# Head 0 of an expert layer: the first eight experts searched and gathered by themselves, and eight scalings spread among the first rows

## The chip, the cores and the metric

The kernel runs on one core of a Trainium2 chip. The metric is the device time of one execution in microseconds; three executions of the kernel before gave a median of 1569.95.

## The reference, cut to what matters

One encoder block over 512 tokens of width 1024, all float32:

```
h   = x + W_out [ FoX attention || differential attention ]( W_in RMSNorm(x) )
hn  = RMSNorm(h)
q   = (hn @ w_q)  as 8 heads x 2 sides x 128
sc  = q against 128 sub keys of each head and side
s1, i1 = top_k(sc[side 0], 16);  s2, i2 = top_k(sc[side 1], 16)
cand   = s1[:, None] + s2[None, :]          (16 x 16 sums)
top_s, pos = top_k(cand, 16);  eidx = i1*128 + i2 at pos
hid = gelu(u_tab[eidx] . hn) * softmax(top_s)
h   = h + sum over 8 heads x 16 experts of hid * v_tab[eidx];  out = RMSNorm(h)
```

The best eight of the 256 sums can only be made of the best eight of each side (a sum at places i and j, counted from 1, has at least i*j sums that are no smaller). So an 8 x 8 table gives the first eight experts of a head, in order.

## The kernel before

The 512 tokens are four tiles of 128 (tokens on the partitions). Work runs in three stages.

1. Tile 0 goes through the attention block alone, up to the queries and keys of its first three heads (the list `BEFORE`).
2. The hosted stage: VectorE (DVE) works through tile 0's experts, 8 heads x 16, one 128x1024 dot product (`dot`, L1489) and one 128x1024 scaled addition (`add_row`, L1525) for each. Between them it does the pieces of the list `AFTER`: the remaining queries and keys of tile 0, and the whole attention block of tiles 1 to 3. TensorE (PE) and ScalarE (ACT) walk the same list. Each head has 4 groups of 4 experts and 9 gaps in a group; `share(p)` gives each piece a weight, and the running sum of weights sets its gap. ACT reaches the gelu of a group (`gelu`, L1138) at gap 6, behind every piece that stands earlier, so a gelu waits for the PE work of those pieces.
3. The last stage: tiles 1 to 3, 24 heads x 16 experts; every row of 8 KB per token (u and v side by side, 1 MB for 128 tokens) is gathered into a ring, DVE makes the dot products, and PE adds the rows (L946).

Expert rows come by indirect DMA that POOL issues (`gather_u` L656, `gather_v` L663, queue q0 of the profile), 512 KB for 128 tokens. The rings hold four u rows and four v rows: a gather of row c waits until row c-4 has been used. POOL issues u0 to u3, and then u4, v0, u5, v1 and so on. Weights come as slabs of 1 MB that SP issues (L597, queue q1) into a ring of two places; the slab after next is issued when the matmuls of a place's present slab are over. A slab of queries serves one head.

Head 0 has a start of its own on DVE: `hn_tile(0)`, then `topk_all(0, 0)` (the whole search of head 0, L1414 to L1474, `topk_first` and the nine parts of `topk_second`), then `later_cols()`: x of tiles 1 to 3, laid out by dimension, is scaled into `actT` by eight instructions of 128x384 (L1623). PE needs all eight (`cols_ready`) before the first projection of tiles 1 to 3 (L740). The searches of later heads lie between the rows of the head ahead.

POOL's first gather waits for the count `TK_IDX` of `topk_step`, which the last instruction of the search of the numbers (L1472, `eidx`) reaches.

Of the kernel before, what the change touches and what calls it, by code (L numbers as in the profile page):

```python
# [25 lines left out]
U32 = mybir.dt.uint32  # L26
ALU = mybir.AluOpType
# [51 lines left out]
def build(nc, x, x_cols, g1_cols, first_halves, slabs, f_cols, b_f, lambda_q1, lambda_k1, lambda_q2, lambda_k2, subln_g,  # L79
# [12 lines left out]
    SLAB = HALF_BANK  # L92
    CHUNK = 64
# [73 lines left out]
    def share(p):  # L167

        kind, tiles = p[0], len(GROUPS[p[1]]) if len(p) > 1 and p[0] != "attend" else 1
        if kind == "attend":  # L170
            _, g, half, step = p
            each = (len(items_of(half)) + VALUES_LAG) / (2 * len(items_of(half)))
            ends = [at_step(g, half, step), at_step(g, half, step - VALUES_LAG)]
            return sum(each * SHARE_ATTEND[e[0]] for e in ends if e)
        if kind == "outproj":
            return SHARE_ROWS[1]
        if kind in ("project", "query"):
            by_rows = in_rows(p[1], p[2]) if kind == "project" else tiles == 1
# [3 lines left out]
        return {"norm1": 4, "xT": 2, "forget": 6, "mix": 4, "mixT": 1, "turn": 1, "selq": 2, "norm2": 4, "hT": 2, "lambda": 1, "lamrow": 1, "squares": 0, "factors": 0, "keys": 1.0 * tiles}[kind]  # L182
# [77 lines left out]
    BEFORE, later = first_pieces[:cut_at], first_pieces[cut_at:] + pieces_of(1)  # L260
# [75 lines left out]
    with ExitStack() as ctx:  # L336
# [82 lines left out]
        eidx = [sb(f"eidx{i}", [P, TOPK], I32) for i in range(3)]  # L419
        gneg = sb("gneg", [P, 1])  # L420
# [87 lines left out]
        topk_step = sem("topk_step")  # L508
        gexp_done = sem("gexp_done")
# [131 lines left out]
        def _(pool):  # L641
# [43 lines left out]
            numbers_of(0)  # L685
            for c in range(COLS):
                gather_u(0, c)
            for n in range(PH * HOSTS):
                for c in range(TOPK):
                    ahead = TOPK * n + c + COLS  # L690
                    if ahead < HOSTED:
                        if ahead % TOPK == 0:
                            numbers_of(n + 1)
                        gather_u(ahead // TOPK, ahead % TOPK)
# [516 lines left out]
        def _(dve):  # L1211
# [32 lines left out]
            def piece(kind, *p):  # L1244
# [12 lines left out]
                elif kind == "factors":  # L1257
# [3 lines left out]
                    for t in range(later):  # L1261
                        nc.vector.tensor_scalar(factor_diag[:, t * P:(t + 1) * P], ident[:, :], stat1[:, 2 * later + t:2 * later + t + 1],
                                                None, ALU.mult).then_inc(factors_ready, 1)
                elif kind == "forget":
# [140 lines left out]

            def topk_first(n, par):
# [8 lines left out]
                for q in range(2):  # L1415
                    after(q + 1)
                    nc.vector.match_replace(tk_w[:, q, :], tk_v[:, q, 0:8], s1[q], -HUGE).then_inc(topk_step, 1)
                for q in range(2):
                    nc.vector.max_index(tk_i[:, q, 0:8], tk_v[:, q, 0:8], s1[q]).then_inc(topk_step, 1)
                for q in range(2):  # L1420
                    after(q + 3)
# [8 lines left out]
            def topk_second(n, par, part):  # L1430
# [37 lines left out]
                else:  # L1468
# [3 lines left out]
                    nc.vector.scalar_tensor_tensor(out=eidx[n % 3][:, :], in0=picked[:, 0, :], scalar=float(K1), in1=picked[:, 1, :],  # L1472
# [144 lines left out]
            def later_cols():  # L1617

                dve.wait_ge(cols_in, 16 * later)
                dve.wait_ge(*emptied(("factors",)))  # L1620
                rows = factor_rows.rearrange("p (t n) -> p t n", t=later)
                for c in range(KC):
                    nc.vector.scalar_tensor_tensor(out=actT[:, c, :].rearrange("p (t n) -> p t n", t=later),  # L1623
                                                   in0=v_all[:, 1:TILES, c * P:(c + 1) * P], scalar=g1c[:, c:c + 1], in1=rows,
                                                   op0=ALU.mult, op1=ALU.mult).then_inc(cols_ready, 1)

            hn_tile(0)
            topk_all(0, 0)
            later_cols()
# [89 lines left out]
```

## Time and profile before

| what | value |
|---|---|
| median of 3 executions (lowest, highest) | 1569.95 us (1568.25, 1570.33) |
| the profiled execution, its own time | 1568.42 us |
| its span in the profile | 1566.6 us |
| PE busy | 1256.3 us, 80% |
| DVE busy | 1142.4 us, 73% |
| POOL busy | 777.5 us, 50% |
| ACT busy | 431.6 us, 28% |
| DMA | 596.49 MB, mean 381 GB/s |

Times in the profile are counted from the start of the span; 1.8 us of the execution's time lie outside of it. Stage 1 ends at about 94 us, stage 2 at about 580 us. The busy shares are averages over stages with different limits.

### The profile page before, as it was taken

To read this page: it belongs to the slowest core of one execution; us is meant where nothing else is said; L and a number is where in the kernel's file an instruction comes from. 1 tells how busy PE (TensorE), PEld (TensorE's weight loads), DVE (VectorE), ACT (ScalarE), POOL (GpSimd) and SP (SyncE) were. 2 spreads that over 40 slices of the span, in tenths; PEclk is the share of its full clock that TensorE was granted. 3 is DMA by queue.
4 is the path that set the end of the run, shared out by engine and by line. 5 is a ranking of instruction groups with operands and counts; after the bars stand their busy time and mean duration, and the time that the engine had idled before them with its cause. 6 is when DMAs were issued, how large, how long until landed. Compare 5 with 4: busy or idle time off the path is not lost.

```text
span 1566.6 us, 12915 instructions
## 1 busy us (share of the span) xinstructions
PE 1256.3 (80%) x3663; PEld 655.4 (42%) x3663; DVE 1142.4 (73%) x2681; ACT 431.6 (28%) x1045; POOL 777.5 (50%) x650
## 2 busy tenths in 40 slices
PE   9988988897775928989987768687777777777777
PEld 8666654475452613444433323233333333333333
DVE  3357799999999888666676776767666776666664
ACT  3321334343441313222221222222222322222122
POOL 0025576776566773444454445444544454445540
PEclk9999988998787968999999989989999999989999
DMA  9479898998789999999999999999999999999994
GB/s 383 183 284 383 338 345 322 373 364 318 277 286 330 368 374 412 421 422 415 421 422 421 421 422 421 421 421 422 421 421 422 421 421 422 421 421 421 422 421 206
DMA packets 102045, 596.49 MB, mean 381 GB/s; under 512 B 11736, under 2 KB 11736, under 8 KB 46680
## 3 DMA queue, kind: packets, MB, share of 16 engines
q0 software_dynamic: 92160, 536.91, 85.2%
q1 hardware_dynamic: 9816, 58.76, 9.5%
q8 instruction: 31, 0.51, 0.1%
q14 instruction: 38, 0.31, 0.1%
HBM read 593.53 MB, written 2.10 MB: 380 GB/s over the span
## 4 chain that ended last, share of the span: by engine, by line
DMA 33%; DVE 15%; PE 12%; ACT 2%; issue 2%; POOL 1%; POOLq 0%; DVEq 0%
PE acc L946 11%; DMA map_mem<-in_peer_uv_dram,eidx 6%; DMA mix_mem<-in_peer_uv_dram,eidx 6%; DMA v_ring<-in_peer_uv_dram,eidx 5%; DMA u_ring<-in_peer_uv_dram,eidx 4%; DMA v_all<-in_peer_uv_dram,eidx 4%; DMA w_ring<-in_peer_uv_dram,eidx 3%; DMA act_mem<-in_peer_uv_dram,eidx 3%; DVE v_ring L1497 1%; PE mm L740 1%; DVE v_all L1497 1%; DVE map_mem L1497 1%; DVE u_ring L1497 1%; DVE onehot L1457 1%; DVE onehot L1463 1%
## 5 line engine op out<-in xcount | busy, mean ns | idle before, releaser
L656 POOL DMA_INDIRECT u_ring<-in_peer_u_dram,eidx x128 | 163.4, 1277 | 177.2 <-DVE gneg L1474 98.7
L1138 ACT ACTIVATE gel<-hid 128x4 f32<-128x4 f32 x126 | 26.1, 207 | 778.8 <-DVE hid L1497 694.9
L663 POOL DMA_INDIRECT v_ring<-in_peer_v_dram,eidx x128 | 154.9, 1210 | 76.5 <-DVE h L1525 44.6
L946 PE MATMUL acc<-v_all,diag 128*128 128x512 f32 x240 | 124.4, 667 | 68.1 <-ACT diag L1145 68.1
L1525 DVE SCALAR_TENSOR_TENSOR h<-v_ring,coef,h 128x1024 f32<-128x1024 f32 x128 | 164.5, 1285 | 7.2 <-DMA v_ring<-in_peer_v_dram,eidx 3.7
L1489 DVE CUSTOM_DVE_ANT_0 u_ring<-u_ring,hn 128x1024 f32<-128x1024 f32 x128 | 156.2, 1220 | 14.5 <-DMA u_ring<-in_peer_u_dram,eidx 12.6
L946 PE MATMUL acc<-v_ring,diag 128*128 128x512 f32 x240 | 116.6, 631 | 29.6 <-ACT diag L1145 29.6
L946 PE MATMUL acc<-u_ring,diag 128*128 128x512 f32 x240 | 116.9, 633 | 28.9 <-ACT diag L1145 28.9
L946 PE MATMUL acc<-map_mem,diag 128*128 128x512 f32 x240 | 113.7, 618 | 23.0 <-ACT diag L1145 23.0
L1145 ACT ACTIVATE diag<-ident,coef 128x128 f32<-128x128 f32 x376 | 121.7, 392 | 27.7 <-DVE coef L1515 21.7
L677 POOL DMA_INDIRECT v_all<-in_peer_uv_dram,eidx x60 | 70.7, 1178 | 92.7 <-PE acc L946 87.7
L740 PE MATMUL mm<-act_mem,w_ring 128*128 128x384 f32 x336 | 115.5, 500 | 0.7 <-ACT act_mem L1065 0.7
L677 POOL DMA_INDIRECT u_ring<-in_peer_uv_dram,eidx x60 | 72.1, 1201 | 86.7 <-PE acc L946 78.7
L677 POOL DMA_INDIRECT map_mem<-in_peer_uv_dram,eidx x60 | 71.0, 1184 | 83.4 <-PE acc L946 77.0
L946 PEld LDWEIGHTS acc<-v_all,diag 128*128 128x128 f32 x240 | 49.9, 213 | 137.3 <-issue 103.0
L1497 DVE CUSTOM_DVE_ANT_0 map_mem<-map_mem,hn 128x1024 f32<-128x1024 f32 x60 | 72.9, 1224 | 45.7 <-DMA map_mem<-in_peer_uv_dram,eidx 45.7
L677 POOL DMA_INDIRECT v_ring<-in_peer_uv_dram,eidx x60 | 70.6, 1176 | 70.7 <-PE acc L946 62.6
L946 PE MATMUL acc<-act_mem,diag 128*128 128x512 f32 x168 | 83.0, 640 | 25.2 <-ACT diag L1145 25.2
L1497 DVE CUSTOM_DVE_ANT_0 v_all<-v_all,hn 128x1024 f32<-128x1024 f32 x60 | 72.9, 1225 | 40.1 <-DMA v_all<-in_peer_uv_dram,eidx 40.1
L1497 DVE CUSTOM_DVE_ANT_0 u_ring<-u_ring,hn 128x1024 f32<-128x1024 f32 x58 | 70.4, 1223 | 41.4 <-DMA u_ring<-in_peer_uv_dram,eidx 41.3
L1497 DVE CUSTOM_DVE_ANT_0 v_ring<-v_ring,hn 128x1024 f32<-128x1024 f32 x58 | 70.3, 1224 | 38.4 <-DMA v_ring<-in_peer_uv_dram,eidx 38.3
L946 PE MATMUL acc<-w_ring,diag 128*128 128x512 f32 x168 | 77.9, 607 | 19.1 <-ACT diag L1145 19.1
(273 smaller groups left out, 2342.4 us busy)
## 6 DMA issues: line engine op xcount, KB each, us to landing
w_ring<-in_slabs_dram SPq DMA_DIRECT2D x37, 1024.0 KB
v_ring<-in_slabs_dram SPq DMA_DIRECT2D x6, 1024.0 KB, 10.8
u_ring<-in_slabs_dram SPq DMA_DIRECT2D x4, 1024.0 KB, 13.0
h<-in_x_dram SPq DMA_DIRECT2D x4, 512.0 KB, 12.9
u_ring<-in_peer_u_dram,eidx POOLq DMA_INDIRECT x128
v_ring<-in_peer_v_dram,eidx POOLq DMA_INDIRECT x128
v_all<-in_x_cols_dram SPq DMA_DIRECT2D x3, 512.0 KB, 6.6
out_dram<-fin SPq DMA_DIRECT2D x3, 512.0 KB
```

The costliest lines, as they stand in the source:

```text
L656: nc.gpsimd.indirect_dma_start(out=u_ring[:, c % U_RING, :], out_offset=None, in_=peer_u[0], in_offset=bass.IndirectOffsetOnAxis(ap=eidx[n ...
L663: nc.gpsimd.indirect_dma_start(out=v_ring[:, c % V_RING, :], out_offset=None, in_=peer_v[0], in_offset=bass.IndirectOffsetOnAxis(ap=eidx[n ...
L677: nc.gpsimd.indirect_dma_start(out=row_mem[place], out_offset=None, in_=peer_uv, in_offset=bass.IndirectOffsetOnAxis(ap=eidx[n % 3][:, c:c ...
L740: last = nc.tensor.matmul(bk[:, 0:n], w[:, c, q * P:(q + 1) * P], actT[:, c, 0:n], start=(c == 0), stop=(c == KC - 1))
L946: last = nc.tensor.matmul(acc[half][:, :], diag[:, c % COLS, :], v_row(n, c)[:, half * BANK:(half + 1) * BANK], start=first, stop=(n % PH ...
L1138: nc.scalar.activation(gel[:, par, g0:g0 + COLS], hid[:, par, g0:g0 + COLS], ACT.Gelu).then_inc(gelu_done, 1)
L1145: nc.scalar.activation(diag[:, c, :], ident[:, :], ACT.Copy, scale=coef[:, par, g0 + c:g0 + c + 1]).then_inc(diag_done, 1)
L1457: nc.vector.tensor_tensor(out=onehot[:, :, :], in0=top_hl[:, :, :].rearrange("p a b -> p (a b)").unsqueeze(2).broadcast_to([P, 2 * TOPK, T ...
L1463: nc.vector.tensor_tensor(out=oh, in0=oh, in1=tk_i[:, :, :].unsqueeze(2).broadcast_to([P, 2, TOPK, TOPK]), op=ALU.mult).then_inc(topk_step, 1)
L1489: nc.vector.tensor_tensor_reduce(out=u_ring[:, c % U_RING, :], in0=u_ring[:, c % U_RING, :], in1=hn[:, :], scale=1.0, scalar=0.0, op0=ALU. ...
L1497: nc.vector.tensor_tensor_reduce(out=u_row(n, c), in0=u_row(n, c), in1=hn[:, :], scale=1.0, scalar=0.0, op0=ALU.mult, op1=ALU.add, accum_o ...
L1525: nc.vector.scalar_tensor_tensor(out=ht, in0=v_ring[:, c % V_RING, :], scalar=coef[:, par, c:c + 1], in1=ht, op0=ALU.mult, op1=ALU.add).th ...
```

## The change

Three things are done.

- In `topk_first`, the search for the numbers of each side's best eight (`max_index`) moves ahead of `match_replace`, for every head; the counts of `topk_step` in the waits follow.
- For head 0 alone, `eight_first()` comes directly behind it: nine instructions on small tiles (an 8x8 table of sums, `max`, `max_index`, two splits of the position, a comparison, a product, a sum, and the numbers themselves) write `eidx[0][:, 0:8]` and raise `first_eight`. POOL's first gather waits for that; it waits for the full search only ahead of u8. The full search of head 0 then writes numbers 8 to 15 only.
- `later_cols()` goes. Its eight instructions are pieces `("cols", 1, i)` of weight 0, one behind each of the first eight pieces of the list `AFTER`. All other pieces keep their gaps.

```
-    BEFORE, later = first_pieces[:cut_at], first_pieces[cut_at:] + pieces_of(1)
+    BEFORE, later = first_pieces[:cut_at], []
+    for i, p in enumerate(first_pieces[cut_at:]):
+        later += [p] + [("cols", 1, i)] * (i < KC)
+    later += pieces_of(1)
...
-            numbers_of(0)
+            pool.wait_ge(first_eight, 1)
             for c in range(COLS):
                 gather_u(0, c)
             for n in range(PH * HOSTS):
                 for c in range(TOPK):
                     ahead = TOPK * n + c + COLS
                     if ahead < HOSTED:
+                        if ahead == EIGHT:
+                            numbers_of(0)
...
+                elif kind == "cols":
+                    g, c = p
+                    dve.wait_ge(cols_in, 16 * later)
+                    dve.wait_ge(*emptied(("factors",)))
+                    rows = factor_rows.rearrange("p (t n) -> p t n", t=later)
+                    nc.vector.scalar_tensor_tensor(out=actT[:, c, :].rearrange("p (t n) -> p t n", t=later),
+                                                   in0=v_all[:, 1:TILES, c * P:(c + 1) * P], scalar=g1c[:, c:c + 1], in1=rows,
+                                                   op0=ALU.mult, op1=ALU.mult).then_inc(cols_ready, 1)
...
+            def eight_first():
+
+                def sides(ap, last):
+
+                    return ap.unsqueeze(last).broadcast_to([P, EIGHT, EIGHT])
+
+                cf = first_cand[:, :, :].rearrange("p a b -> p (a b)")
+                link(nc.vector.tensor_tensor(out=first_cand[:, :, :], in0=sides(tk_v[:, 0, 0:EIGHT], 2), in1=sides(tk_v[:, 1, 0:EIGHT], 1),
+                                             op=ALU.add))
+                link(nc.vector.max(first_v[:, :], cf))
+                link(nc.vector.max_index(first_p[:, :], first_v[:, :], cf))
+                nc.vector.tensor_scalar(first_hl[:, 0, :], first_p[:, :], 3, None, ALU.logical_shift_right).then_inc(dve_chain, 1)
+                chain[0] += 1
+                link(nc.vector.tensor_scalar(first_hl[:, 1, :], first_p[:, :], EIGHT - 1, None, ALU.bitwise_and))
...
+                nc.vector.scalar_tensor_tensor(out=eidx[0][:, 0:EIGHT], in0=first_id[:, 0, :], scalar=float(K1), in1=first_id[:, 1, :],
+                                               op0=ALU.mult, op1=ALU.add).then_inc(first_eight, 1)
...
                 for q in range(2):
                     after(q + 1)
+                    nc.vector.max_index(tk_i[:, q, 0:8], tk_v[:, q, 0:8], s1[q]).then_inc(topk_step, 1)
+                if n == 0:
+                    after(4)
+                    eight_first()
+                for q in range(2):
                     nc.vector.match_replace(tk_w[:, q, :], tk_v[:, q, 0:8], s1[q], -HUGE).then_inc(topk_step, 1)
                 for q in range(2):
-                    nc.vector.max_index(tk_i[:, q, 0:8], tk_v[:, q, 0:8], s1[q]).then_inc(topk_step, 1)
-                for q in range(2):
-                    after(q + 3)
+                    after(q + 5)
...
-                    nc.vector.scalar_tensor_tensor(out=eidx[n % 3][:, :], in0=picked[:, 0, :], scalar=float(K1), in1=picked[:, 1, :],
+                    lo = EIGHT if n == 0 else 0
+                    nc.vector.scalar_tensor_tensor(out=eidx[n % 3][:, lo:], in0=picked[:, 0, lo:], scalar=float(K1), in1=picked[:, 1, lo:],
...
             hn_tile(0)
             topk_all(0, 0)
-            later_cols()
```

On DVE, at the head of head 0's search, the rows before were:

```order
L1532 SCALAR_TENSOR_TENSOR hn<-h,rstd,g2b 128x1024
L1414 MAX tk_v<-store 128x8 x2
L1417 MATCH_REPLACE tk_w<-tk_v,store 128x128 x2
L1419 MAX_INDEX tk_i<-tk_v,store 128x8 x2
L1422 MAX tk_v<-tk_w 128x8 x2
```

and in the changed kernel they are (L1434 to L1448 are `eight_first`):

```order
L1459 MAX tk_v<-store 128x8 x2
L1462 MAX_INDEX tk_i<-tk_v,store 128x8 x2
L1434 TENSOR_TENSOR first_cand<-tk_v 128x64
L1436 MAX first_v<-first_cand 128x8
L1437 MAX_INDEX first_p<-first_v,first_cand 128x8
L1438 TENSOR_SCALAR first_hl<-first_p 128x8
L1440 TENSOR_SCALAR first_hl<-first_p 128x8
L1441 TENSOR_TENSOR first_hot<-first_hl,iota_i 128x128
L1445 TENSOR_TENSOR first_hot<-first_hot,tk_i 128x128
L1447 TENSOR_REDUCE first_id<-first_hot 128x16
L1448 SCALAR_TENSOR_TENSOR eidx<-first_id 128x8
L1467 MATCH_REPLACE tk_w<-tk_v,store 128x128 x2
```

Nine instructions have come in, and the remaining search of head 0 stands behind them.

On DVE, at the end of that search and among the first four dot products (`u_ring`), the rows before were:

```order
L1472 SCALAR_TENSOR_TENSOR eidx<-picked 128x16
L1474 TENSOR_SCALAR gneg<-top_v 128x1
L1623 SCALAR_TENSOR_TENSOR act_mem<-v_all,g1c,fin 128x384 x8
L1489 ISA u_ring,hid<-u_ring,hn 128x1024
L1489 ISA hid 128x1
```

and now the scalings (L1282) stand one, three, two and two behind the four dot products:

```order
L1521 SCALAR_TENSOR_TENSOR eidx<-picked 128x8
L1523 TENSOR_SCALAR gneg<-top_v 128x1
L1538 ISA u_ring,hid<-u_ring,hn 128x1024
L1538 ISA hid 128x1
L1282 SCALAR_TENSOR_TENSOR act_mem<-v_all,g1c,fin 128x384
L1538 ISA u_ring,hid<-u_ring,hn 128x1024
L1538 ISA hid 128x1
L1282 SCALAR_TENSOR_TENSOR act_mem<-v_all,g1c,fin 128x384 x3
...
L1282 SCALAR_TENSOR_TENSOR act_mem<-v_all,g1c,fin 128x384 x2
L1530 RECIPROCAL gsum<-gsum 128x1
```

On POOL, at its first gathers, what each waits for was (u0 to u3, u4, v0, u5):

```order
L656 DMA u_ring<-in_peer_u_dram,eidx0 128x1024 [waits topk_step]
L656 DMA u_ring<-in_peer_u_dram,eidx0 128x1024 x3
L656 DMA u_ring<-in_peer_u_dram,eidx0 128x1024 [waits dot_done]
L663 DMA v_ring<-in_peer_v_dram,eidx0 128x1024
L656 DMA u_ring<-in_peer_u_dram,eidx0 128x1024 [waits dot_done]
```

and it is now (u0 to u3, u4, then u8 and v4):

```order
L667 DMA u_ring<-in_peer_u_dram,eidx0 128x1024 [waits first_eight]
L667 DMA u_ring<-in_peer_u_dram,eidx0 128x1024 x3
L667 DMA u_ring<-in_peer_u_dram,eidx0 128x1024 [waits dot_done]
...
L667 DMA u_ring<-in_peer_u_dram,eidx0 128x1024 [waits dot_done,topk_step]
L674 DMA v_ring<-in_peer_v_dram,eidx0 128x1024 [waits v_used]
```

The order of the gathers is as before; the first waits for another count, and u8 for one more. The sequences on PE, ACT and SP are as before.

## Rows read from the trace of the kernel before

**Rows 1.** Busy time by stretch: PE, PEld, DVE, ACT, POOL, then PEclk, DMA share, GB/s

```profile
100.00:104.00 4.00, 3.92 (x22) 3.40 (x21) 3.93 (x10) 1.31 (x4) 2.17 (x2) 1.00 0.66 227
110.00:144.00 34.00, 26.04 (x99) 19.27 (x99) 22.84 (x58) 7.43 (x21) 18.80 (x17) 0.90 1.02 413
```

**Rows 2.** The same view of the longer stretches

```profile
182.00:560.00 378.00, 307.65 (x1218) 198.08 (x1216) 356.61 (x746) 138.80 (x276) 257.09 (x206) 0.87 0.90 329
700.00:1500.00 800.00, 632.50 (x1358) 267.81 (x1359) 557.81 (x1407) 189.85 (x498) 383.43 (x320) 0.93 1.01 421
```

**Rows 3.** Timeline of DVE, head 0's search: start, us, instruction, [idle before <- releaser]

```profile
93.58 0.49 DVE L1414 MAX8 tk_v<-store 128x8 f32<-128x128 f32 x2 [1.46 <-ACT store L1099]
...
95.93 0.40 DVE L1426 TENSOR_TENSOR cand<-tk_v 128x256 f32<-128x256 f32 x1
96.37 0.43 DVE L1440 MAX8 top_v<-cand 128x8 f32<-128x256 f32 x1
...
98.15 0.42 DVE L1450 FIND_INDEX8 top_p<-top_v,onehot 128x8 uint32<-128x256 f32 x1
98.61 0.17 DVE L1453 TENSOR_SCALAR top_hl<-top_p 128x16 uint32<-128x16 uint32 x1
...
99.62 0.69 DVE L1463 TENSOR_TENSOR onehot<-onehot,tk_i 128x512 f32<-128x512 f32 x1
...
101.06 0.17 DVE L1472 SCALAR_TENSOR_TENSOR eidx<-picked 128x16 int32<-128x16 f32 x1
...
101.22 4.31 DVE L1623 SCALAR_TENSOR_TENSOR act_mem<-v_all,g1c,fin 128x384 f32<-128x384 f32 x8
```

**Rows 4.** Timeline of DVE, the first, third and fourth dot product of head 0

```profile
107.33 1.23 DVE L1489 CUSTOM_DVE_ANT_0 u_ring<-u_ring,hn 128x1024 f32<-128x1024 f32 x1 [1.80 <-DMA u_ring<-in_peer_u_dram,eidx]
...
114.01 1.23 DVE L1489 CUSTOM_DVE_ANT_0 u_ring<-u_ring,hn 128x1024 f32<-128x1024 f32 x1 [3.59 <-DMA u_ring<-in_peer_u_dram,eidx]
...
117.29 1.23 DVE L1489 CUSTOM_DVE_ANT_0 u_ring<-u_ring,hn 128x1024 f32<-128x1024 f32 x1 [2.05 <-DMA u_ring<-in_peer_u_dram,eidx]
```

**Rows 5.** Timeline of POOL, the gathers of u0 and u3

```profile
101.52 1.27 POOL L656 DMA_INDIRECT u_ring<-in_peer_u_dram,eidx  x1 [98.73 <-DVE gneg L1474]
...
106.65 0.94 POOL L656 DMA_INDIRECT u_ring<-in_peer_u_dram,eidx  x1 [0.30 <-issue]
```

**Rows 6.** Timeline of DVE, its waits for the second gelu and for the forget gates

```profile
123.98 0.14 DVE L1515 TENSOR_TENSOR coef<-gel,gate 128x4 f32<-128x4 f32 x1
...
141.71 0.16 DVE L1515 TENSOR_TENSOR coef<-gel,gate 128x4 f32<-128x4 f32 x1 [5.22 <-ACT gel L1138]
...
182.55 0.60 DVE L1273 TENSOR_SCALAR z_f<-mm,bf 8x384 f32<-8x384 f32 x1 [3.53 <-PE mm L791]
```

**Rows 7.** Timeline of ACT, the gelus of head 0's first two groups

```profile
122.02 0.21 ACT L1138 ACTIVATE gel<-hid 128x4 f32<-128x4 f32 x1
...
141.09 0.49 ACT L1038 ACTIVATE store<-acc 128x384 f32<-128x384 f32 x1 [4.69 <-PE acc L740]
141.48 0.20 ACT L1138 ACTIVATE gel<-hid 128x4 f32<-128x4 f32 x1
```

**Rows 8.** Timeline of PE: queries of heads 4, 5, 7, and the first projection

```profile
105.99 3.62 PE L732 MATMUL mm<-w_ring,store 128*128 128x256 f32 x16
...
113.92 5.38 PE L732 MATMUL mm<-w_ring,store 128*128 128x256 f32 x16 [3.38 <-issue]
...
128.34 5.38 PE L732 MATMUL mm<-w_ring,store 128*128 128x256 f32 x16 [3.73 <-issue]
...
135.73 5.33 PE L740 MATMUL acc<-act_mem,w_ring 128*128 128x384 f32 x16
```

**Rows 9.** Timeline of SP, the issues of the slabs of heads 4, 5, 7

```profile
100.84 0.33 SPq L597 DMA_DIRECT2D w_ring<-in_slabs_dram  x1
105.25 0.33 SPq L597 DMA_DIRECT2D w_ring<-in_slabs_dram  x1
119.32 0.33 SPq L597 DMA_DIRECT2D w_ring<-in_slabs_dram  x1
```

**Rows 10.** DMA queues from 118 to 122 us: packets, MB, share of 16 engines

```profile
q0 software_dynamic: 456, 1.65, 102.8%
```

More of the change, by code:

```diff
@@ L92, in build @@
     SLAB = HALF_BANK
+    EIGHT = 8
     CHUNK = 64
@@ L181, in share @@
             return SHARE_ROWS[0] if by_rows else SHARE_COLS[0] + SHARE_COLS[1] * tiles
-        return {"norm1": 4, "xT": 2, "forget": 6, "mix": 4, "mixT": 1, "turn": 1, "selq": 2, "norm2": 4, "hT": 2, "lambda": 1, "lamrow": 1, "squares": 0, "factors": 0, "keys": 1.0 * tiles}[kind]
+        return {"norm1": 4, "xT": 2, "forget": 6, "mix": 4, "mixT": 1, "turn": 1, "selq": 2, "norm2": 4, "hT": 2, "lambda": 1, "lamrow": 1, "squares": 0, "factors": 0, "cols": 0, "keys": 1.0 * tiles}[kind]
     def woven(a, b):
@@ L419, in build @@
         eidx = [sb(f"eidx{i}", [P, TOPK], I32) for i in range(3)]
+        first_cand = sb("first_cand", [P, EIGHT, EIGHT])
+        first_v = sb("first_v", [P, EIGHT])
+        first_p = sb("first_p", [P, EIGHT], U32)
+        first_hl = sb("first_hl", [P, 2, EIGHT], U32)
+        first_hot = sb("first_hot", [P, 2 * EIGHT, EIGHT])
+        first_id = sb("first_id", [P, 2, EIGHT])
         gneg = sb("gneg", [P, 1])
@@ L508, in build @@
         topk_step = sem("topk_step")
+        first_eight = sem("first_eight")
         gexp_done = sem("gexp_done")
@@ L1404, in after_topk @@
                 dve.wait_ge(topk_step, TK * n + k)
+            def eight_first():
[9 more added lines that the diff above has]
+                link(nc.vector.tensor_scalar(first_hl[:, 1, :], first_p[:, :], EIGHT - 1, None, ALU.bitwise_and))
+                link(nc.vector.tensor_tensor(out=first_hot[:, :, :],
+                                             in0=first_hl[:, :, :].rearrange("p a b -> p (a b)").unsqueeze(2).broadcast_to([P, 2 * EIGHT, EIGHT]),
+                                             in1=iota_i[:, 0:EIGHT].unsqueeze(1).broadcast_to([P, 2 * EIGHT, EIGHT]), op=ALU.is_equal))
+                hot = first_hot[:, :, :].rearrange("p (a b) c -> p a b c", a=2)
+                link(nc.vector.tensor_tensor(out=hot, in0=hot, in1=tk_i[:, :, 0:EIGHT].unsqueeze(2).broadcast_to([P, 2, EIGHT, EIGHT]),
+                                             op=ALU.mult))
+                link(nc.vector.tensor_reduce(first_id[:, :, :].rearrange("p a b -> p (a b)"), first_hot[:, :, :], AX, ALU.add))
+                nc.vector.scalar_tensor_tensor(out=eidx[0][:, 0:EIGHT], in0=first_id[:, 0, :], scalar=float(K1), in1=first_id[:, 1, :],
+                                               op0=ALU.mult, op1=ALU.add).then_inc(first_eight, 1)
             def topk_first(n, par):
@@ L1615, in next_head @@
                     topk_gates(n + 1, 1 - par)
[L1617 to L1625, printed above, removed]
             hn_tile(0)
             topk_all(0, 0)
-            later_cols()
             for tile in range(HOSTS):
```

## The prediction

> **What bounds the kernel now.** I read the busy time by stretch first, then the timelines of DVE, POOL, ACT, PE and SP around the place of the change, and last the DMA queues there.
>
> The last stage is bound by DMA: from 700 to 1500 us the engines' share is 1.01 at 421 GB/s [rows 2]. It moves a fixed number of bytes, so its end moves with its start, and that start comes when DVE has come through the hosted stage. In the hosted stage from 182 to 560 us DVE is busy 356.61 of 378.00 us [rows 2], 94%. So from 182 us on, a shift of DVE's place passes on to the end nearly whole. What sets DVE's place at 182 us is another matter: there DVE has stood 3.53 us waiting for PE's matmul of the forget gates [rows 6]. That PE work stands in one unbroken run behind the first projection of tiles 1 to 3, which starts at 135.73 us [rows 8]. Hence the question that decides this change is not when head 0's rows arrive, but whether PE starts that projection at another time.
>
> What PE waits for ahead of it are slabs. The queries of head 5 begin at 113.92 after 3.38 us of idle time, those of head 7 at 128.34 after 3.73 us [rows 8]; the profile names no engine ("issue"), and what the program has there is the wait for the slab. SP issued these slabs at 105.25 and 119.32 [rows 9], so from issue to use they took 8.7 and 9.0 us. The slab of head 4 was issued at 100.84 [rows 9] and used at 105.99 without a wait [rows 8], 5.15 us at most. The difference is the gathers: from 110 to 144 us the DMA engines are full (share 1.02, 413 GB/s), from 100 to 104 they are not (0.66, 227 GB/s) [rows 1].
>
> **The change, part by part.**
>
> *Eight first: added.* Nine small DVE instructions. From start to start the search's table of 256 sums took 96.37 - 95.93 = 0.44 us, `MAX8` of 256 elements 0.43, `FIND_INDEX8` 98.61 - 98.15 = 0.46, a split 0.17 and a product over 512 elements 0.69 [rows 3]. The new ones have 64, 64, 64, 8, 8, 128, 128, 128 and 8 elements. Upper end: all at these prices, 0.44 + 0.43 + 0.46 + 0.17 x 2 + 0.69 x 3 + 0.17 = 3.9 us. Lower end: nine at 0.17, 1.5 us. `MAX8` of 128 elements took 0.49 / 2 = 0.25 [rows 3], so the time falls with the size, and I take 0.22 + 0.20 + 0.33 + 0.28 + 3 x 0.30 + 0.17 = 2.1 us. The numbers of each side's best eight move forward, 0.5 us. Ready: 93.58 + 0.5 (two `MAX8`) + 0.5 + 2.1 = 96.7; POOL starts 0.3 us behind that, as it did (101.06 + 0.17 = 101.23, then 101.52) [rows 3, 5]: **96.9 instead of 101.5, 4.6 us earlier**.
>
> *The rest of the search.* Its end goes from 101.23 to 101.23 + 2.1 = 103.3, which delays nothing but u8 on POOL (behind a DVE wait anyway) and ACT's exponential of the gates, which no instruction waits for ahead of the first coefficients.
>
> *The scalings: moved.* 4.31 us for eight [rows 3]. Before they lay in the time in which u0 was on its way (DVE still waited 1.80 us afterwards [rows 4]), so they cost nothing. Now u0, if it lands 107.33 - 101.52 = 5.8 us behind POOL's start as before [rows 4, 5], is there at 102.7, ahead of DVE at 103.3. The scalings then lie between dots 0 to 3, where DVE waited for u2 3.59 and for u3 2.05 us [rows 4], and cover the same kind of wait. With no wait at all dots 0 to 3 and eight scalings take 4 x 1.2 + 4.3 = 9.1 us, to 112.4; with some of the wait for u2 and u3 left I expect 114, against 117.29 + 1.23 = 118.5 before. So DVE is 4 to 5 us ahead there.
>
> *Where the lead goes.* DVE then needs about 5.5 us (search of head 1, dot 4) to the first coefficients, which it read at 123.98 without waiting [rows 6]. ACT's first gelu stood at 122.02 [rows 7], behind the copies of head 5's queries, whose matmuls began at 113.92 and took 5.38 us [rows 8]; it didn't wait for the dots but for PE. So DVE now reaches the coefficients at about 119.5 to 120 and must wait until 122.2: of 4.5 us of lead some 1.7 are left. The second gelu stood at 141.48, directly behind the copy of the first projection at 141.09 [rows 7], and DVE waited 5.22 us for it [rows 6]. It will wait about 7 instead and go on at 141.7 as before. **The whole lead is gone at 141.7, unless PE has moved.**
>
> *Does PE move?* The scalings are no obstacle: they are over by 115, PE needs them at 135.73. The slabs can move.
> Gain, upper bound: the DMA engines fill the room they had from 100 to 104, 4 x (413 - 227) GB/s = 0.74 MB, which is 1.8 us at 413 GB/s [rows 1]. If the shorter or shifted idle times of PE spare one stretch at the lower clock (5.38 against 3.62 us for the same 16 matmuls [rows 8]), 1.76 us more: 3.6 us.
> Against it: SP issues a slab only when PE has finished with its place, and head 7's slab took 9.0 us while queue q0 alone filled the engines from 118 to 122 (102.8%) [rows 10]. In the changed kernel q0 still has gathers queued there: of the twelve rows ahead of u8, POOL has issued all by about 115, 6.3 MB together with three slabs of 3.1 MB since 97 are 23 us at 413 GB/s, so until 120 or later. As long as q0 is never dry, a slab sees the same competition however early the gathers began.
> Loss: the slab of head 4 (issued 100.84) had little company and now has four gathers. At half of 413 GB/s 1.05 MB take 5.1 instead of 2.5 us, so head 4's queries begin up to 2.5 us late, the slab of head 6 is issued at 112.1 instead of 105.99 + 3.62 = 109.6, and after 9 us is there at 121.1. PE used it at about 120 (113.92 + 5.38 and two short pieces), so head 6 is 1.1 us late. The slab of the first projection is issued when head 6 is done, and PE may be 1.1 us late at 135.73.
> The Trainium skill ("DMA: Bandwidth & Descriptors", section on queues, rings and completion order) says that a DMA engine goes round robin between the queue rows that have work, one packet at a time, and this is a rule against this change: by it, gathers put beside head 4's slab take a share from it at once, and the sum would be that +1.1. The trace agrees as far as it goes (5.15 us without company, 8.7 and 9.0 with it).
> I take -0.5: between -1.8 and +1.1, a little on the side of the gain, since filled room is certain, and who gets it is not.
>
> *Sum.* -4.6 (gathers) absorbed by the gelu waits, +2.1 and 4.3 us of DVE work in place of waits, 0; PE -0.5. Profiled execution: span 1566.1, with 1.8 outside 1567.9. It stood 1.5 us below the median (1568.42 against 1569.95), so the median comes to **1569.4**.
>
> **The rivals.**
>
> *PE comes earlier.* Room in the DMA engines and one stretch of full clock reach the first projection: -1.8 to -3.6, and with both slow stretches spared -5.3; also near to it the naive sum, in which the gathers' 4.6 us pass through whole. For it: both idle times of PE are waits for slabs, and behind each the same 16 matmuls took 5.38 instead of 3.62 us [rows 8], the lower clock. Against it: the slab's own 9 us. Time 1566.3. It shows as a first projection that starts before 134.
>
> *Slower: the slabs come later.* Place: head 4's slab, then head 6's, then that of the first projection. Price +1.1 as worked out, and with one more idle time that drops the clock 1.76 more: +2.9; a loss beyond 0.2% needs both slow stretches to grow. It decides once PE's first projection starts after 136.8. Time 1572.8.
>
> *The gathers don't come that much earlier.* POOL's work for a gather took 1.27 us beside DVE's scalings and 0.94 for u3 [rows 5]; it now lies beside the search. Even at 2 us for each of four, the lead shrinks by some 3 us and still ends in the same wait: no change in the time. The Trainium skill ("SBUF — State Buffer", who interferes with whom) says that descriptor generation on GpSimd is shut out while DVE runs in a two-port mode, which `tensor_scalar` can be; only a few such instructions, of 0.17 us [rows 3], lie there.
>
> **How the numbers follow.** 0.2% of the time is 3.1 us, about what a measurement of this kernel can tell from no change. Absorbed, within -1.5 to +1: 0.60, the likeliest, own range 1568.4 to 1571. PE earlier, 0.28, of which 0.22 reach beyond 3.1 us. Slabs later, 0.12, of which 0.07 reach beyond. So faster 0.22, within 0.71, slower 0.07. The range takes in -3.9 to +3.1: 1566.0 to 1573.0.
>
> **What would show it.** First gather on POOL at about 97; `eight_first` some 2 us; search over at 103.3; dots 0 to 3 over by 114; first coefficients behind a wait of about 2 us for the gelu at 122; second coefficients at about 141.7 after a wait of about 7; first projection between 134.5 and 136.8. Slabs 9 us from issue to use where PE waits for them. I am wrong if the projection starts elsewhere, or if DVE's place at 182.55 does not carry over to the end of the hosted stage one for one.

## The result and the profile after

The changed kernel is slower: median 1571.52 us of 21 runs against 1568.25 of 21 runs of the kernel before, ratio 1.0023 with a 95% interval of 1.0012 to 1.0034. I had forecast no change to be told (1569.4, range 1566.0 to 1573.0), and given slower 7%. The time lies within the range, but with some luck: the range was counted from a median of 1569.95 of three runs, and the 21 runs gave 1568.25, so the shift is +3.27 us, just beyond the +3.1 that the range allowed. The direction was not forecast. Single runs of one kernel spread by 10 to 14 us (1559.32 to 1573.51 before, 1565.97 to 1576.35 now), so the 0.23% is one of medians.

The profiled execution took 1571.52 us, span 1569.4 (before 1568.42, 1566.6). POOL's timeline of the changed kernel shows the first gathers: start, us, instruction, [idle before <- releaser].

```profile
97.10 1.09 POOL L667 DMA_INDIRECT u_ring<-in_peer_u_dram,eidx  x1 [94.30 <-DVE eidx L1448]
...
100.99 0.94 POOL L667 DMA_INDIRECT u_ring<-in_peer_u_dram,eidx  x1 [0.30 <-issue]
```

They start 4.4 us earlier than in [rows 5], and u3 5.7 us earlier. DVE's timeline of the changed kernel has what answers to [rows 3, 4, 6]: the first eight numbers, the first and fourth dot product, the coefficients of groups 1 and 2, and the forget gates.

```profile
96.65 0.17 DVE L1448 SCALAR_TENSOR_TENSOR eidx<-first_id 128x8 int32<-128x8 f32 x1
...
103.47 1.22 DVE L1538 CUSTOM_DVE_ANT_0 u_ring<-u_ring,hn 128x1024 f32<-128x1024 f32 x1
...
113.73 1.23 DVE L1538 CUSTOM_DVE_ANT_0 u_ring<-u_ring,hn 128x1024 f32<-128x1024 f32 x1 [1.46 <-DMA u_ring<-in_peer_u_dram,eidx]
...
123.78 0.16 DVE L1564 TENSOR_TENSOR coef<-gel,gate 128x4 f32<-128x4 f32 x1 [2.03 <-ACT gel L1151]
...
146.17 0.16 DVE L1564 TENSOR_TENSOR coef<-gel,gate 128x4 f32<-128x4 f32 x1 [9.85 <-ACT gel L1151]
...
187.00 0.60 DVE L1294 TENSOR_SCALAR z_f<-mm,bf 8x384 f32<-8x384 f32 x1 [4.08 <-PE mm L804]
```

DVE is 3.9 us ahead at dot 0 and 3.6 at dot 3. At the first coefficients it waits 2.03 us and is level with before (123.78 against 123.98); at the second it waits 9.85 us and is 4.5 us behind (146.17 against 141.71), and so it comes to the forget gates, 187.00 against 182.55. DVE's own work has not grown by that much; PE, for whom ACT's gelu waits, is late. PE's timeline of the changed kernel, heads 3 to 7 and the first projection, against [rows 8]:

```profile
101.49 3.62 PE L745 MATMUL mm<-w_ring,store 128*128 128x256 f32 x16
...
110.20 6.23 PE L745 MATMUL mm<-w_ring,store 128*128 128x256 f32 x16 [4.16 <-issue]
...
117.20 3.62 PE L745 MATMUL mm<-w_ring,store 128*128 128x256 f32 x16
...
125.09 5.38 PE L745 MATMUL mm<-w_ring,store 128*128 128x256 f32 x16 [3.34 <-issue]
...
131.23 3.62 PE L745 MATMUL mm<-w_ring,store 128*128 128x256 f32 x16
...
138.40 7.12 PE L753 MATMUL acc<-act_mem,w_ring 128*128 128x384 f32 x16 [1.37 <-DMA w_ring<-in_slabs_dram]
```

Before, heads 5 and 7 waited for their slabs, 3.38 and 3.73 us. Now heads 4 and 6 and the first projection wait, 4.16, 3.34 and 1.37 us. Behind every wait the same matmuls run slower: 6.23, 5.38 and 7.12 us, where without a wait they take 3.62, 3.62 and 5.33. Windows of the changed kernel over the beginning of these stretches, with one over head 5, which didn't wait (the window; PE, PEld, DVE, ACT and POOL busy with their counts; granted clock of TensorE; DMA share; GB/s):

```profile
110.20:113.00 2.80, 2.80 (x7) 2.27 (x8) 2.07 (x4) 0.00 (x0) 1.22 (x2) 0.50 1.01 417
117.20:120.00 2.80, 2.80 (x15) 2.47 (x14) 2.77 (x16) 0.63 (x3) 0.35 (x1) 1.00 1.04 417
125.10:128.00 2.90, 2.90 (x8) 2.38 (x9) 2.90 (x7) 0.00 (x0) 2.09 (x2) 0.58 0.90 370
138.40:141.00 2.60, 2.60 (x6) 1.43 (x7) 0.00 (x0) 0.00 (x0) 0.00 (x0) 0.66 1.04 432
```

A granted clock of 0.50 is the lower level, 1.2 GHz, and 1.00 is 2.4 GHz; 0.58 and 0.66 are stretches partly at each. Head 5 has 1.00, the three behind a wait don't. The sum is 8.87 us of waiting and 6.16 of slow clock against 7.11 and 3.52 before: 15.0 against 10.6, and the difference of 4.4 us is the 4.45 us at the forget gates. 2.64 of it are clock. In the second pair of profiles (below) the same sums are 11.8 against 8.0, and 1.79 of the 3.8 us are clock. So some half of the loss at the gates is clock, and how much differs from execution to execution.

The DMA queues from 102 to 104 us show where it began (packets, MB, share of 16 engines), in the kernel before:

```profile
q1 hardware_dynamic: 72, 0.59, 71.7%
```

and in the changed kernel:

```profile
q0 software_dynamic: 168, 0.62, 85.6%
q1 hardware_dynamic: 3, 0.02, 3.1%
```

Head 4's slab was issued at 100.84 before and at 100.76 now. Before it had the engines to itself and moved 0.59 MB in these two microseconds; now the gathers of u0 to u3 are at work and it moves 0.02. It came into use 9.4 us behind its issue, not 5.15.

This late start is no matter of head 4's slab alone. Head 6's slab was issued at 116.46 in the changed kernel, and the DMA queues from 117 to 119 us show only gathers:

```profile
q0 software_dynamic: 224, 0.82, 102.2%
```

It had moved 0.03 MB by 120. In the kernel before head 7's slab was issued at 119.32, and in [rows 10] the gathers' queue stands alone up to 122. So each of these three slabs moved next to nothing for about 3 us behind its issue.

At the end of the hosted stage 3.3 of the 4.45 us are left in this pair of profiles: POOL's timeline has the first gather of the last stage (`v_all`) at 578.40, and in the kernel before it is at 575.12.

```profile
578.40 1.22 POOL L688 DMA_INDIRECT v_all<-in_peer_uv_dram,eidx  x1 [0.30 <-issue]
```

### The profile page after: what moved, and what is told of

The parts are those of the page before. It is cut to its first block, busy times and chain, and to the rows that moved or that the text cites. A ratio compares the mean times of both kernels' runs of the same rounds, so it can differ in the third digit from the quotient of the medians.

```text
span 1569.4 us, 12933 instructions
## 1 busy us (share of the span) xinstructions
PE 1267.6 (81%) x3663; PEld 660.6 (42%) x3663; DVE 1145.2 (73%) x2691; ACT 431.0 (27%) x1045; POOL 774.1 (49%) x650
## 4 chain that ended last, share of the span: by engine, by line
DMA 32%; PE 15%; DVE 13%; ACT 2%; issue 2%; POOL 1%; DVEq 0%
PE acc L959 13%; DMA map_mem<-in_peer_uv_dram,eidx 7%; DMA u_ring<-in_peer_uv_dram,eidx 6%; DMA act_mem<-in_peer_uv_dram,eidx 6%; DMA w_ring<-in_peer_uv_dram,eidx 5%; DMA mix_mem<-in_peer_uv_dram,eidx 3%; DMA v_ring<-in_peer_uv_dram,eidx 3%; DMA v_all<-in_peer_uv_dram,eidx 3%; PE mm L753 2%; DVE u_ring L1546 1%; DVE map_mem L1546 1%; DVE v_ring L1546 1%; DVE act_mem L1546 1%; ACT diag L1158 1%; DVE v_all L1546 1%
## 5 line engine op out<-in xcount | busy, mean ns | idle before, releaser
L959 PE MATMUL acc<-v_all,diag 128*128 128x512 f32 x240 | 127.9, 683 | 68.6 <-ACT diag L1158 68.6
L959 PE MATMUL acc<-map_mem,diag 128*128 128x512 f32 x240 | 120.2, 648 | 29.3 <-ACT diag L1158 29.3
L688 POOL DMA_INDIRECT map_mem<-in_peer_uv_dram,eidx x60 | 74.7, 1246 | 87.8 <-PE acc L959 80.3
```

Of the source, the lines that this page charges most:

```text
L688: nc.gpsimd.indirect_dma_start(out=row_mem[place], out_offset=None, in_=peer_uv, in_offset=bass.IndirectOffsetOnAxis(ap=eidx[n % 3][:, c:c ...
L959: last = nc.tensor.matmul(acc[half][:, :], diag[:, c % COLS, :], v_row(n, c)[:, half * BANK:(half + 1) * BANK], start=first, stop=(n % PH ...
```

## The experiments

Theory 1: the early gathers take the DMA engines from head 4's slab, and PE, which waits on slabs, comes late to the first projection. Rival 2: DVE's 2.1 us of added work, or the scalings among the rows, are what costs. Rival 3: it isn't the bytes, but the presence of any work in the gathers' queue. Of every run I read the start of PE's first projection, of the forget gates on DVE, and the ratio to the kernel before on the same chip. The numbers behind "Measured" are that ratio, its 95% interval and the median; the places come from the one execution that was profiled.

**The first gather waits for the full search** (the changed kernel, everything else kept):

```
             pool.wait_ge(first_eight, 1)
+            numbers_of(0)
```

> The changed kernel, but POOL's first gather waits for the full search again; the nine small instructions and the spread scalings stay. Theory 1 (the early gathers take DMA time from head 4's slab, and the order of PE's waits turns over): head 4's queries start at 105.9 without a wait, PE waits at heads 5 and 7 as before, the first projection starts at 135.7 (within 0.5), the forget gates on DVE at 182.5; time that of before within 0.1%. Rival 2 (the added 2.1 us of DVE work, or the scalings among the rows, are what costs): first projection late, near 138.4, time 0.2% above before, as in the changed kernel.

Measured: 0.9974 (0.9958 to 0.9989), 1563.0 us. Not the time of before, but faster than both kernels. PE's timeline of this kernel:

```profile
105.88 3.62 PE L746 MATMUL mm<-w_ring,store 128*128 128x256 f32 x16
111.06 3.69 PE L746 MATMUL mm<-w_ring,store 128*128 128x256 f32 x16 [0.64 <-ACT qyT L1106]
117.69 5.38 PE L746 MATMUL mm<-w_ring,store 128*128 128x256 f32 x16 [2.00 <-issue]
...
131.63 7.12 PE L754 MATMUL acc<-act_mem,w_ring 128*128 128x384 f32 x16 [2.00 <-DMA w_ring<-in_slabs_dram]
```

Gathers start at 104.42, 2.9 us later than before. Now heads 4 and 5 both have their slabs in time, the first projection comes at 131.63 and the forget gates at 180.23. Rival 2 falls: all of DVE's added work is there, and the loss is not. My expectation of the pattern was wrong too, since I had taken the pattern of before for the undisturbed one; it was already disturbed.

**The early search alone**: the pieces `("cols", 1, i)` go, `later_cols()` stands behind the search again.

> The changed kernel, but the eight scalings stand in one block behind the search, as before. Theory 1: the gathers still start at 97, so head 4's queries wait until about 110, the first projection starts at about 138.4, the forget gates come at about 187; time 0.2% above before. Rival 2 with the scalings as the cause: first projection at 135.7, time that of before.

Measured: 1.0033 (1.0017 to 1.0049), 1572.14 us. First projection at 139.28, forget gates at 187.61. The early search alone brings a loss as large as that of the changed kernel.

**The spread scalings alone**, in the kernel before:

```
-    BEFORE, later = first_pieces[:cut_at], first_pieces[cut_at:] + pieces_of(1)
+    BEFORE, later = first_pieces[:cut_at], []
+    for i, p in enumerate(first_pieces[cut_at:]):
+        later += [p] + [("cols", 1, i)] * (i < KC)
+    later += pieces_of(1)
...
-            later_cols()
```

> The kernel before with the eight scalings spread behind the first dots, nothing else. The gathers start at 101.5 as before. Theory 1: head 4 without a wait, first projection at 135.7, forget gates at 182.5, time within 0.1% of before. Rival 2: the first projection later, and a time up to 0.2% above before.

Measured: 1.0005 (0.9989 to 1.0021), 1567.66 us; first projection 134.93, forget gates 181.75. No difference that these runs can tell, as theory 1 had it; a loss of the size of 1.0023 lies outside the interval.

**u2 waits for head 4's slab**, in the changed kernel:

```
+            fourth = slab_order.index((0, N_IN + N_OUT + 4))
             for c in range(COLS):
+                if c == 2:
+                    pool.wait_ge(slab_in[slab_place(fourth)[0]], 16 * slab_count(fourth))
                 gather_u(0, c)
```

> The changed kernel, but POOL issues only u0 and u1 early and waits ahead of u2 until head 4's slab has landed. Theory 1: half of the competition is gone, head 4's slab lands between 106 and 108, PE waits there 0 to 2 instead of 4.2 us; if it is near 106, the order of waits turns back (heads 5 and 7) and the first projection starts at 135 to 136.5, time that of before within 0.1%. Rival 2: no difference to the changed kernel, first projection at 138.4. Rival 3 (what counts is any early gather, since a slab issued while queue q0 is at work starts late): head 4 still waits 3 us or more.

Measured: 1.0011 (0.9995 to 1.0028), 1568.04 us. Head 4 begins at 108.14 after a wait of 2.03 us, the first projection at 133.55, the forget gates at 182.16. Half the competition, half the wait. Whether the loss is gone the times don't say: the interval holds 1 as well as the 1.0023 of the changed kernel. The pattern didn't turn back to heads 5 and 7 (heads 4 and 6 and the projection wait, about 2 us each), and the first projection, which I had put at 135 to 136.5, came at 133.55. The half wait speaks against rival 3.

**The first four gathers bring 128 of 1024 columns**, in the changed kernel (the first four dot products of head 0 are made of other data):

```
+                few = P if n == 0 and c < U_RING else D
-                    out=u_ring[:, c % U_RING, :], out_offset=None, in_=peer_u[0],
+                    out=u_ring[:, c % U_RING, 0:few], out_offset=None, in_=peer_u[0],
```

> The changed kernel, but the first four gathers (u0 to u3) bring only 128 of 1024 columns, so head 0's first four dot products are made of other data; instructions and waits are the same. Theory 1 (it is the bytes beside head 4's slab): head 4's slab lands by 107 and PE waits there under 1.5 us instead of 4.2; first projection at 131 to 136. Rival 3 (it is the number of descriptors or the mere presence of work in queue q0): head 4 waits 3 us or more, as in the changed kernel.

Measured: 0.9999 (0.9986 to 1.0012), 1565.92 us. The gathers start at 97.05 with the same number of rows, and heads 4 and 5 have their slabs without a wait. PE's timeline of this kernel, heads 4 to 6:

```profile
105.83 3.62 PE L746 MATMUL mm<-w_ring,store 128*128 128x256 f32 x16
110.22 3.62 PE L746 MATMUL mm<-w_ring,store 128*128 128x256 f32 x16
118.27 5.21 PE L746 MATMUL mm<-w_ring,store 128*128 128x256 f32 x16 [3.50 <-issue]
```

The first projection comes at 131.60 after 1.57 us of wait, the forget gates at 180.18. In the DMA queues from 100 to 104 us the slabs move 0.92 MB here beside 0.20 of gathers; in the changed kernel it is 0.19 beside 1.11. So what the gathers move beside the slab is the cause (bytes and the packets that carry them, which fell together from 301 to 96), not the number of rows or the mere presence of work, and rival 3 falls. The interval lies below that of the changed kernel's (1.0012 to 1.0034), if only just. The time is that of before, though the forget gates come 2.4 us earlier than in the first profile of before; the second profile of before has them at 180.01, so this is no gain that needs a cause. The profiled execution was also the fastest of its ten (1562.73). What is left unexplained is that PE's path is the same as in the first experiment (131.63 and 180.23 there), while the median lies 0.25% higher.

**All gathers held until head 4's slab has landed**, in the kernel before:

```
             numbers_of(0)
+            fourth = slab_order.index((0, N_IN + N_OUT + 4))
+            pool.wait_ge(slab_in[slab_place(fourth)[0]], 16 * slab_count(fourth))
```

> The kernel before, but POOL waits ahead of u0 until head 4's slab has landed, so that the gathers begin at about 105 instead of 101.5; nothing on DVE changes. Theory 1: later gathers leave the slabs of heads 4 and 5 alone, PE waits less, first projection at 131 to 133, time 3 to 5 us below before, like the run in which the changed kernel waited for the full search. Rival 2 (that run gained by something on DVE, its nine instructions or the spread scalings): time of before.

Measured: 0.9995 (0.9983 to 1.0007), 1565.74 us. A miss: I had expected 3 to 5 us. Heads 4 and 5 don't wait, but head 6 waits 2.81 and the projection 2.38 us, and it runs at the lower clock:

```profile
118.89 5.17 PE L734 MATMUL mm<-w_ring,store 128*128 128x256 f32 x16 [2.81 <-issue]
...
132.99 8.36 PE L742 MATMUL acc<-act_mem,w_ring 128*128 128x384 f32 x16 [2.38 <-DMA w_ring<-in_slabs_dram]
```

The profiled execution is the slowest of the twelve (1569.16). All of PE's work from about 70 us on lies 1.2 us later in it than in the profile of the kernel before (head 1 at 94.00 against 92.80), well ahead of what was changed, and the gathers start at 107.63. From head 1 to the first projection it takes 38.99 us, and in the first experiment 38.90, with waits at the same two places; what is longer is the slow stretch behind it, 8.36 against 7.12. So the path of PE is the one that theory 1 forecast, and the time is not: by its number this run is what its rival 2 foretold (time of before), and the gain of the first experiment over both kernels is not shown to come from the later gathers. That rival (the gain comes from something on DVE) stays open. The interval overlaps that of the first experiment by 0.06%. Holding the gathers is no sure gain.

**The slabs of heads 0, 1, 4 and 5 early**, in the kernel before. This is no test of the loss, but of whether slabs set the time. The rings of the expert rows lie idle until head 0's gathers; the query slabs of heads 0 and 1 go into the u ring, those of heads 4 and 5 into the v ring, and the gathers that overwrite them wait for their matmuls:

```
-EARLY_SLABS = 16
+EARLY_SLABS = 22
...
+            def slab_over(place):
+                m = max(m for m in range(EARLY_SLABS) if m % EARLY_PLACES == place)
+                pool.wait_ge(mm_full, slab_last_use[slab_order[m]] + 1)
...
             def gather_u(n, c):
+                if n == 0 and c < U_RING and c % 2 == 0:
+                    slab_over(4 + c // 2)
...
             def gather_v(n, c):
+                if n == 0 and c < V_RING and c % 2 == 0:
+                    slab_over(2 + c // 2)
```

> The kernel before, but the query slabs of heads 0 and 1 go into the u ring, those of heads 4 and 5 into the v ring, which lie idle until head 0's gathers, so that SP can issue all of them by about 86 us (the DMA engines stand still from 88 to 92). POOL waits for the matmuls of those slabs ahead of u0, u2, v0 and v2. Theory 1 (PE's slab waits set the time): PE goes through heads 3 to 7 with at most one short wait, the first projection starts between 125 and 130 instead of 135.7, the forget gates come up to 8 us earlier, and the time is 4 to 8 us below before (0.3 to 0.5%). Rival (DVE or DMA become the bound at once): the first projection moves, the time by less than 0.1%.

Measured: 0.9944 (0.9924 to 0.9963), 1557.25 us, the fastest of all. PE's timeline of this kernel:

```profile
105.88 3.62 PE L741 MATMUL mm<-v_ring,store 128*128 128x256 f32 x16
110.27 3.62 PE L741 MATMUL mm<-v_ring,store 128*128 128x256 f32 x16
114.65 3.62 PE L741 MATMUL mm<-w_ring,store 128*128 128x256 f32 x16
119.97 3.62 PE L741 MATMUL mm<-w_ring,store 128*128 128x256 f32 x16
127.67 6.96 PE L749 MATMUL acc<-act_mem,w_ring 128*128 128x384 f32 x16 [1.91 <-DMA w_ring<-in_slabs_dram]
```

Heads 4 to 7 run without a wait and at full clock, the first projection starts 8.1 us earlier than in the first profile of before (5.5 than in the second), the forget gates come at 176.12, 6.4 us earlier (3.9), and the time is 0.56% less, some 9 us (1557.25 against 1566.37 for the kernel before on the same chip). That is a little more than the 4 to 8 us that I had forecast, and more than PE's gain at the gates explains; the interval (0.37 to 0.76%) is wide, with seven runs. The rival falls.

**The same early slabs in the changed kernel**:

> The changed kernel with the same early slabs as in the run with the kernel before. Theory 1: with head 4's and 5's slabs landed before the gathers start at 97, the early gathers have little left to hinder; first projection between 125 and 130, time 4 to 8 us below before, and no longer behind the same version without the early search. Rival: gathers from 97 on still delay the slabs of heads 6, 7 and of the projection, and it stays 2 to 3 us behind that version.

Measured: 0.9967 (0.9955 to 0.9978), 1560.98 us. First projection at 128.62, forget gates at 175.53. With the slabs out of the way the early gathers cost PE nothing that these profiles show (this profile is of the fastest of its twelve executions, 1556.97). They gain nothing either: the median is 3.7 us above that of the version without them, measured beside the same runs of before. The rival had 2 to 3 us, and the intervals of the two just overlap. So whether the early search still costs something there stays open.

**The early slabs with the spread scalings, without the early search**:

> The kernel before with the query slabs of heads 0, 1, 4 and 5 early in the u and v rings, and with the spread scalings, but without the early search. Theory 1: as the version with the early slabs alone, time 0.4 to 0.6% below before, since the scalings only lie where DVE waits anyway. Rival (DVE's lead counts once the slabs are out of the way): 1 us or more below that version.

Measured: 0.9957 (0.9939 to 0.9975), 1562.31 us. First projection at 129.47, forget gates at 177.94, in the slowest of its eight executions (1565.81). As the other two within the intervals; no gain from DVE's lead shows, though one of 1 us, which the rival asked for, could hide in intervals of this width.

**Each kernel profiled once more.**

> The kernel before once more, for how far one profile repeats. Theory 1: the pattern of PE's waits is a property of the kernel: heads 5 and 7 wait for their slabs, the first projection starts 42.9 us behind head 1's queries within 1 us, the forget gates 89.8 behind them. Rival: the pattern is chance and differs from execution to execution by several us, and then no single pair of profiles explains the difference.

> The changed kernel once more. Theory 1: heads 4 and 6 and the first projection wait, the first projection starts 45.7 us behind head 1's queries within 1 us, the forget gates 94.3 behind them. Rival: another pattern than in its first profile.

Measured: the same heads wait in both. The kernel before has its first projection at 133.20 and the forget gates at 180.01 (head 7 waited 2.74 us this time, and no slow stretch followed: 3.69 us). The changed kernel has them at 136.82 and 183.74. So the pattern belongs to the kernel, the length and above all the clock behind each wait do not: one more profile moved the gates by 2.5 and 3.3 us, more than the 1 us that I had allowed. In both pairs the changed kernel is the later one, by 4.45 and 3.73 us. The lateness at the gates doesn't reach the end in every pair: of these two executions that of the changed kernel was the shorter, 1567.11 against 1568.42 us, since the kernel before lost 5.9 us more between the gates and the last stage. The loss itself rests on the medians of 21 runs each.

Over the kernel before, the changed one and the nine others that were timed in rounds, the place of the forget gates in the profile (175.53 to 187.61) and the time (ratio times 1568) go together: a line through the eleven points has a slope of 1.03 us per us, correlation 0.92. The scatter about it is some 2 us, as much as a second profile moves the place. Each place is from one execution and each time a median of many, so this shows that the two go together over the kernels, no more.

## Why the prediction was wrong

**What bounds the kernel** was right as far as the runs show. Over the kernels the end follows DVE's place at the forget gates (slope 1.03), and that place is PE's, which is set by slabs and by the clock behind each wait for one. I had called it a sign of being wrong if the place at the gates does not carry over one for one; in the first pair of profiles 3.3 of 4.45 us did, in the second none. That DVE's lead does not count was right as well: it was gone at the first coefficients (2.03 us of wait, about 2 forecast) and turned into a longer wait at the second.

**The prices on DVE and POOL** held: the nine instructions from 94.55 to 96.82, 2.3 us (2.1 forecast); first gather at 97.10 (96.9); end of the search at 103.5 (103.3); dots 0 to 3 over at 115.0 (114).

**The step that failed** is "Does PE move?", where I took -0.5 between -1.8 and +1.1. PE moved by +2.67 at the first projection, and with its slow stretch by +4.45 at the gates (+3.62 and +3.73 in the second pair). Three things in it:

- The loss on head 4's slab: up to 2.5 us by an equal share of the engines. It was 4.16. Before it moved 0.59 MB from 102 to 104, now 0.02, so it did not get half at once. The rows of the prediction held this already: head 7's slab was issued at 119.32 [rows 9], and queue q0 alone moved until 122 [rows 10], which is no share for 2.7 us. The Trainium skill ("DMA: Bandwidth & Descriptors", queues, rings and completion order) has the engines go round robin between queues packet by packet; the trace agrees from 104 us on, where both queues move side by side, as the DMA queues from 104 to 106 us in the changed kernel show:

```profile
q1 hardware_dynamic: 58, 0.48, 58.3%
q0 software_dynamic: 79, 0.30, 39.2%
```

  From 105 to 107 us it is 67 packets of the slabs with 0.55 MB against 68 of the gathers with 0.26: one for one in packets, and by bytes two to one for the slab, whose packets are larger. For the 3 us ahead of that the trace shows no turns. Whether the slab's queue had no work ready for the engines yet, or had it and was passed over, is not settled by any run here. The runs do show what changes it: with short rows in the gathers head 4's slab moved 0.11 MB between 101 and 102, as in the kernel before (0.07), and with u2 held it began at about 103.
- What the delay does further on. The two places of the slab ring make two chains: a slab is issued when the head two places ahead is done, comes 8 to 9 us later if gathers are at work (9.4, 8.6 and 7.9 here), and its head's matmuls free the place again. Before, the first slab with company was head 5's (issued 105.25), and PE's way to the projection held two such trips, heads 5 and 7. Now the first is head 4's (issued 100.76), and the way holds three: 110.20, 125.09, 138.40, in steps of 14.9 and 13.3 us. I had carried head 4's delay on as +1.1, as if only the excess over head 5's wait counted, and had argued that a slab sees the same competition however early the gathers start. That holds for the slabs that had company before. Head 4's had none.
- The clock. I had seen that matmuls behind a wait run slower (5.38 against 3.62 us) and used it as a gain that might come. Three waits instead of two gave three slow stretches, 6.16 us instead of 3.52 (in the second pair 3.62 instead of 1.83). The rival "slower: the slabs come later" had the place right, and its +2.9 with one more slow stretch is near the measured +3.3; I had given it 12%, and 7% to a loss that can be told. That its number is so near is in part luck: at the gates the waits had grown by 1.76 us and the slow clock by 2.64, where it had 1.1 and 1.76, and 1.2 us were lost again on the way to the last stage.

The rivals "PE comes earlier" and "the gathers don't come that much earlier" didn't happen: POOL's four gathers took 0.94 to 1.09 us beside the search.

**What stays open.** Between the gates and the last stage's first gather, executions differ by up to 7 us without a pattern by kernel (388.1 us in the run in which the first gather waits for the full search, 395.2 in the second profile of the kernel before). One part is a wait of DVE that the trace puts down to "remote": in the second profile of before 3.6 us, in the first none. DVE's waits in the second profile of before from 190 to 560:

```profile
DVE map_mem L1374 <- remote: 3.6, 1, 3.6
```

It stood in five of the thirteen profiles (1.4 to 3.7 us), and what causes it is not known. Open too is why the first experiment is faster than both kernels, and what the held gathers in the kernel before lack for it.

## What to carry to other kernels

When a transfer starts earlier, look for the transfer that had the DMA engines to itself until then, and for who waits for that one: here a 1 MB weight slab, on which the other engines' progress hung. Don't price the encounter as an equal share from the first moment; look in the trace of before for the same encounter elsewhere, and read there how long the second transfer gets nothing. A ring of two places that is refilled on release turns one late slab into a late slab every second time. Where the memory of a later stage lies idle, loading into it ahead was worth 0.56% here, where starting the later stage's own loads sooner cost 0.23%.

## What the runs showed of the hardware

How soon a slab begins to move depends on the other queue. With the gathers' queue empty, head 4's slab in the kernel before was issued at 100.84 and had moved its first 0.07 MB by 102. With that queue busy, three slabs moved next to nothing for about 3 us: head 4's in the changed kernel (issued 100.76, 0.02 MB by 104), head 6's there (issued 116.46, 0.03 MB by 120) and head 7's in the kernel before (issued 119.32, none by 122). Only then did both queues move side by side, packet for packet.

How long POOL works on a gather depends on what DVE does meanwhile. Beside the block of eight scalings the gathers of u0 to u2 took 1.27, 1.13 and 1.81 us in both profiles of the kernel before; in the kernel with only the scalings spread, at the same place, they took 1.09, 0.94 and 0.94.

TensorE's clock made up about half of the loss at the gates, and it varies. Behind PE idle times of 2.0 to 4.2 us the next head's 16 matmuls mostly took 5.2 to 6.6 us instead of 3.62: behind 2.00 us 5.38 (first gather held for the search), behind 3.61 us 6.62 (spread scalings alone), behind 4.16 us 6.23 (changed kernel). But not every time: behind 2.74 us in the second profile of before, behind 2.84 us with the spread scalings alone and behind 2.03 us with u2 held they took 3.69. Over all profiles they were slow in eleven of eleven cases with 3.06 to 4.16 us of idle time, and in three of six with 2.00 to 2.84. Head 7 in the two profiles of the kernel before, the first (3.73 us idle ahead of it) at 0.58:

```profile
128.40:131.00 2.60, 2.60 (x7) 2.08 (x8) 2.60 (x7) 0.00 (x0) 1.99 (x3) 0.58 1.00 408
```

and the second (2.74 us idle) at the full 2.4 GHz:

```profile
127.50:131.00 3.50, 3.50 (x16) 3.11 (x17) 3.50 (x8) 0.00 (x0) 2.81 (x3) 1.00 1.00 411
```

The Trainium skill ("TensorE: Matmul & The Clock Gate", Part 1) says that the default state is the throttled one and that activity releases it; the runs agree in kind, and show that the length of the wait alone does not decide it here. One such stretch is worth 1.5 to 3.0 us, so one profile of a kernel can't tell a difference of that size.
